# Layer 0 transposes the raw x, applies the inverse norm behind its projection, and takes x, identity and gain from one tensor

## The reference

```python
h = rms_norm(x, attn_norm[0])            # x * rsqrt(mean(x^2) + EPS) * gain, per token
proj = h @ w_in                          # q, k, v (1024 columns each) and 16 forget-gate columns
q = rms_norm(proj[..., :D] per head, qn)
k = rms_norm(proj[..., D:2*D] per head, kn)
v = proj[..., 2*D:3*D]
log_f = log_sigmoid(proj[..., 3*D:] + b_f)
cum = cumsum(log_f) over tokens          # enters the attention logits
```

## Time and profile before

| | us |
|---|---|
| median of 3 runs | 1317.16 |
| lowest and highest | 1314.86, 1318.45 |
| the profiled execution, its own time | 1315.91 |
| its span | 1314.1 |
| PE busy in it | 1295.5 |
| DVE, ACT, POOL busy | 1008.7, 873.4, 458.7 |

### The profile page before, as it was taken

One profiled execution on the slowest core, in us unless ns is written; L12 is line 12 of the kernel. 1 busy time (PEld: TensorE's weight loads), 2 busy tenths in 40 slices (PEclk: granted clock), 3 DMA queues, 4 the chain that ended last, 5 costly groups with the idle time before them and its releaser, 6 DMA issues.

```text
span 1314.1 us, 22109 instructions
## 1 busy us (share of the span) xinstructions
PE 1295.5 (99%) x6964; PEld 1096.7 (83%) x6964; DVE 1008.7 (77%) x1603; ACT 873.4 (66%) x1567; POOL 458.7 (35%) x498
## 2 busy tenths in 40 slices
PE   7999999999999999999998999999999999999998
PEld 5888888888888888888887888888888888888887
DVE  6877898955777788885578789886476888888745
ACT  6776777744667777774467777775367776777533
POOL 3741245410275225552026314552015521555200
PEclk9999999999999999999998999999999999999999
DMA  7734555565664455556451365556455435555651
GB/s 268 237 102 141 174 192 185 189 219 166 203 228 146 148 180 180 191 190 216 168 185 61 115 211 192 187 184 211 163 198 187 144 113 189 183 189 192 213 171 64
DMA packets 64602, 232.39 MB, mean 177 GB/s; under 512 B 7472, under 2 KB 7600, under 8 KB 64528
## 3 DMA queue, kind: packets, MB, share of 16 engines
q1 hardware_dynamic: 61632, 221.35, 50.7%
q0 software_dynamic: 2896, 10.08, 2.5%
HBM read 230.35 MB, written 1.05 MB: 176 GB/s over the span
## 4 chain that ended last, share of the span: by engine, by line
PE 97%; DVE 1%; ACT 1%; DMA 0%; issue 0%; POOL 0%; SPq 0%; DVEq 0%
PE bank L1589 28%; PE bank L1895 25%; PE bank L1898 12%; PE bank L1565 7%; PE bank L1567 6%; PE bank L1566 6%; PE bank L1604 5%; PE bank L1736 2%; PE bank L1759 2%; PE bank L1575 2%; PE bank L1658 1%; DMA w_raw<-weights 0%; PE bank L1683 0%; PE bank L1744 0%; ACT w_hi L457 0%
## 5 line engine op out<-in xcount | busy, mean ns | idle before, releaser
L866 DVE TENSOR_TENSOR w_lo<-w_raw,w_hi 128x1024 fp32r<-128x1024 f32 x418 | 543.3, 1318 | 109.2 <-ACT w_hi L457 107.7
L457 ACT ACTIVATE w_hi<-w_raw 128x1024 fp32r<-128x1024 f32 x418 | 430.2, 1053 | 136.5 <-PE bank L1589 107.5
L1895 PE MATMUL bank<-hT,w_hi 128*128 128x512 f32 x1408 | 444.6, 395 | 0.0
L1898 PEld LDWEIGHTS bank<-hT,w_lo 128*128 128x128 f32 x1408 | 264.5, 188 | 59.7
L1898 PE MATMUL bank<-hT,w_lo 128*128 128x256 f32 x1408 | 281.9, 278 | 0.0
L1550 POOL TENSOR_TENSOR gT_lo<-gate_c,gT_hi 128x256 f32 (+1 forms) x88 | 170.8, 1941 | 201.8 <-ACT gT_hi L818 201.8
L1895 PEld LDWEIGHTS bank<-hT,w_hi 128*128 128x128 f32 x1408 | 216.6, 189 | 3.9 <-issue 1.1
L1381 POOL TENSOR_SCALAR ssq<-ssq 128x1 f32<-128x1 f32 x24 | 12.7, 528 | 361.9 <-ACT tok L483 361.9
L1565 PE MATMUL bank<-w_hi,hT 128*128 128x512 f32 (+1 forms) x336 | 134.3, 400 | 2.0 <-DVE hT L920 2.0
L1567 PE MATMUL bank<-w_hi,hT 128*128 128x512 f32 (+1 forms) x336 | 130.5, 388 | 0.0
L1566 PE MATMUL bank<-w_lo,hT 128*128 128x512 f32 (+1 forms) x336 | 130.4, 388 | 0.0
(11 more groups left out here) (164 smaller groups left out, 1991.1 us busy)
## 6 DMA issues: line engine op xcount, KB each, us to landing
w_raw<-weights SPq DMA_DIRECT2D x418, 512.0 KB, 3.7
gain<-gains POOLq DMA_DIRECT2D x11, 512.0 KB, 4.6
rel<-rel_in POOLq DMA_DIRECT2D x8, 256.0 KB, 4.0
x<-x_in SPq DMA_DIRECT2D x4, 256.0 KB, 4.3
out<-x SPq DMA_DIRECT2D x4, 256.0 KB, 2.0
p_end<-p_in POOLq DMA_DIRECT2D x3, 256.0 KB, 4.9
consts<-consts_in POOLq DMA_DIRECT2D x1, 392.0 KB, 5.2
conv_sb<-conv POOLq DMA_DIRECT2D x1, 352.0 KB, 3.8
```

The lines of the kernel that those rows point to most:

```text
L457: nc.scalar.activation(w_hi[:, slot, q * HALF:(q + 1) * HALF], w_raw[:, raw, :], ACT.Copy).then_inc(hi_ready, 1)
L866: nc.vector.tensor_tensor(w_lo[:, slot, cols], w_raw[:, half(q)[0], :], w_hi[:, slot, cols].bitcast(F32), ALU.subtract).then_inc(lo_ready, 1)
L1895: nc.tensor.matmul(up_banks(L, slot)[:, side, :], w_hi[:, *at(side)], hT[:, c, :, :], start=c == 0, stop=c == KC - 1, skip_group_check=True)
L1898: last = nc.tensor.matmul(up_banks(L, slot)[:, side, 0:SEQ], w_lo[:, *at(side)], hT_hi[:, c, :], start=False, stop=c == KC - 1, skip_group ...
```

## The change

Layer 0's first norm loses its multiplication. PE transposes the raw `x`; ACT and DVE still apply the gain behind the transposes. The inverse norm `rstd` (one number for each token) is applied when q, k and v are copied out of PSUM, as a per-partition scale of the ACT copies (`rstd` for L572 and L587, `rstd_sq` = `rstd` / 8 for the squares of L575), and in the v rest. `rstd_sq` is made by two new POOL instructions ahead of POOL's DMA issues. For the forget gate, whose result has heads on partitions, PE also transposes a broadcast of `rstd` (two more transposes) and DVE multiplies by it (`gate_in` has five instructions instead of two).

Identity, gain and x become one tensor in DRAM (`first_ins`, 8768 bytes a partition row) and one in SBUF (`first_in`); the first of the four x transfers brings gain, identity and 512 columns of x in rows of 2624 bytes, and SP issues two DMAs fewer ahead of the weights. ACT and DVE change order at the start: rounding comes before the split of the same step, the squares of both tiles come after the second unit's split, and tile 1's rounding is interleaved with the fourth unit's halves. The gain buffer's first load no longer waits. `first_in` is 1 KB longer per partition than x was; with `ident`, `gain0` and `qr` gone as tensors of their own, everything placed behind the old `ident` lies 512 bytes higher, and x, tok, hT and gain 1024 bytes; w_raw, w_hi and w_lo stay. `qr` moves into `small`.

```diff
+X_AT = 256
+GAIN0_AT = X_AT - KC - P - 8
-        x = sb("x", [P, TT, D])
+        first_in = sb("first_in", [P, X_AT + TT * D])
+        gain0 = first_in[:, GAIN0_AT:GAIN0_AT + KC]
+        ident = first_in[:, GAIN0_AT + KC:GAIN0_AT + KC + P]
+        x = first_in[:, X_AT:X_AT + TT * D].rearrange("p (t d) -> p t d", t=TT)
...
 # SP
-                    c = slice(b * 512, (b + 1) * 512)
-                    sp.dma_start(x[:, t, c], x_in[t * P:(t + 1) * P, c]).then_inc(x_landed[2 * t + b], 16)
-                if t == 0:
-                    sp.dma_start(ident[:], ident_in).then_inc(ident_landed, 16)
-                    sp.dma_start(gain0[:], gain0_in).then_inc(gain0_landed, 16)
+                    c = slice(X_AT + t * D + b * 512 if t or b else GAIN0_AT, X_AT + t * D + (b + 1) * 512)
+                    sp.dma_start(first_in[:, c], first_ins[:, c.start - GAIN0_AT:c.stop - GAIN0_AT]).then_inc(x_landed[2 * t + b], 16)
...
 # ACT
+            for b in range(2):
+                round_hT(0, 0, parts=(b,))
+                split_hi(0, 0, half_of(0), first=True, halves=(b,))
+            split_hi(1, 1, half_of(1), first=True)
             square(0, 0)
-            for b in range(2):
-                split_hi(0, 0, half_of(0), first=True, halves=(b,))
-                round_hT(0, 0, parts=(b,))
-            split_hi(1, 1, half_of(1), first=True)
             square(0, 1)
             split_hi(2, 2, half_of(2), first=True)
-            split_hi(3, 3, half_of(3), first=True, halves=(0,))
-            round_hT(0, 1)
-            split_hi(3, 3, half_of(3), first=True, halves=(1,))
+            for b in range(2):
+                round_hT(0, 1, parts=(b,))
+                split_hi(3, 3, half_of(3), first=True, halves=(b,))
...
+                    if L == 0:
+                        act.wait_ge(rstd_sq_ready, t + 1)
+                    nc.scalar.activation(qn[:, n % 3, 0:cols], src[:, 0:cols], ACT.Copy,
+                                         scale=1.0 if L else rstd[:, t:t + 1]).then_inc(raw_ready, 1)
+                    nc.scalar.activation(sq[:, 0:cols], src[:, 0:cols], ACT.Square,
+                                         scale=HD ** -0.5 if L else rstd_sq[:, t:t + 1]).then_inc(sq_ready, 1)
...
 # DVE
-            dve.wait_ge(x_landed[0], 16)
-            dve.wait_ge(x_landed[1], 16)
-            normalise(0, 0)
-            dve.wait_ge(gain0_landed, 16)
             for b in range(2):
+                rest_hT(0, 0, parts=(b,))
                 split_lo(0, 0, half_of(0), halves=(b,))
-                rest_hT(0, 0, parts=(b,))
             split_lo(1, 1, half_of(1))
-            normalise(0, 1)
             split_lo(2, 2, half_of(2))
-            split_lo(3, 3, half_of(3), halves=(0,))
-            rest_hT(0, 1)
-            split_lo(3, 3, half_of(3), halves=(1,))
+            for b in range(2):
+                rest_hT(0, 1, parts=(b,))
+                split_lo(3, 3, half_of(3), halves=(b,))
...
+                    if L == 0:
+                        dve.wait_ge(f_done, 1)
+                        own.inc(nc.vector.tensor_copy(fe[:], aux[1][0:HEADS, SEQ:2 * SEQ]))
+                        own.inc(nc.vector.tensor_scalar(fmin[:], aux[1][2 * HEADS:3 * HEADS, 0:SEQ], 0.0, None, ALU.add))
+                        own.wait()
+                        own.inc(nc.vector.tensor_tensor(fz[:], aux[1][0:HEADS, 0:SEQ], fmin[:], ALU.add))
+                        own.wait()
+                        own.inc(nc.vector.tensor_tensor(fmin[:], fz[:], fe[:], ALU.mult))
+                        own.wait()
+                        nc.vector.tensor_scalar(fz[:], fmin[:], bf[:, 0:1], None, ALU.add).then_inc(f_z, 1)
+                        return
...
 # POOL
             norm_rstd(0)
+            for t in range(TT):
+                pool.wait_ge(rstd_ready, t + 1)
+                nc.gpsimd.tensor_scalar(rstd_sq[:, t:t + 1], rstd[:, t:t + 1], HD ** -0.5, 1.0, ALU.mult, ALU.mult).then_inc(rstd_sq_ready, 1)
             pool.dma_start(p_raw(0), p_in[0]).then_inc(p_landed, 16)
...
 # PE
+                    if L == 0:
+                        pe.wait_ge(rstd_ready, TT)
+                        for t in range(TT):
+                            nc.tensor.transpose(aux[1][0:HEADS, SEQ + t * P:SEQ + (t + 1) * P],
+                                                       rstd[:, t:t + 1].to_broadcast([P, HEADS]), ident)
```

More of the change, by code:

```diff
@@ L153, in half_of, with trunk @@
     return lambda q: ((2 * u + q) % RAW, (2 * u + q) // RAW + 1)
-def trunk(nc, weights, x_in, p_in, gains, gain0_in, smalls, gainT_in, bf_in, conv, wf_in, rel_in, ident_in, consts_in, out):
+def trunk(nc, weights, first_ins, p_in, gains, smalls, gainT_in, bf_in, conv, wf_in, rel_in, consts_in, out):
     with ExitStack() as ctx:
@@ L169, in trunk @@
         gain = sb("gain", [P, D])
-        ident = sb("ident", [P, P])
         consts = sb("consts", [P, C_END])
@@ L255, in trunk @@
         sink = small[:, S_SINK:S_END]
+        qr = small[:, S_GAIN:S_GAIN + TT * HEADS].rearrange("p (t h) -> p t h", t=TT)
         def in_bank(i, t):
@@ L316, in trunk @@
         rstd_ready = sem("rstd_ready")
+        rstd_sq_ready = sem("rstd_sq_ready")
         tok_ready = sem("tok_ready")
@@ L586, in evacuate_v @@
                     wait_block(act, L, blk, t)
-                    nc.scalar.activation(v_hi[:, t, c * 512:(c + 1) * 512], in_bank(blk, t)[:, :], ACT.Copy).then_inc(v_hi_ready, 1)
+                    nc.scalar.activation(v_hi[:, t, c * 512:(c + 1) * 512], in_bank(blk, t)[:, :], ACT.Copy,
+                                         scale=1.0 if L else rstd[:, t:t + 1]).then_inc(v_hi_ready, 1)
                 def gate_logs():
@@ L902, in normalise @@
                 dve.wait_ge(rstd_ready, 2 * n + t + 1)
-                if n:
-                    dve.wait_ge(gain_landed, 16 * n)
+                dve.wait_ge(gain_landed, 16 * n)
                 for b in range(2):
                     c = slice(b * 512, (b + 1) * 512)
-                    if n == 0:
-                        nc.vector.tensor_scalar(tok[:, t, c], x[:, t, c], rstd[:, t:t + 1], None, ALU.mult).then_inc(tok_ready, 1)
-                        continue
                     nc.vector.scalar_tensor_tensor(tok[:, t, c], x[:, t, c], rstd[:, t:t + 1], gain[:, c],
@@ L1049, in rest_v @@
                         cols = slice(c * 512, (c + 1) * 512)
-                        ins = nc.vector.tensor_tensor(v_lo[:, t, cols], src[:, :], v_hi[:, t, cols].bitcast(F32), ALU.subtract)
+                        if L == 0:
+                            ins = nc.vector.scalar_tensor_tensor(v_lo[:, t, cols], src[:, :], rstd[:, t:t + 1],
+                                                                 v_hi[:, t, cols].bitcast(F32), ALU.mult, ALU.subtract)
+                        else:
+                            ins = nc.vector.tensor_tensor(v_lo[:, t, cols], src[:, :], v_hi[:, t, cols].bitcast(F32), ALU.subtract)
                     else:
@@ L1365, in load_gain @@
             def load_gain(n):
-                pool.wait_ge(tok_ready, 4 * n)
+                if n > 1:
+                    pool.wait_ge(tok_ready, 4 * (n - 1))
                 pool.dma_start(gain[:], bass.AP(gains.tensor, n * D, [[0, P], [1, D]])).then_inc(gain_landed, 16)
@@ L1571, in transpose_tok @@
                 for b in range(2):
-                    pe.wait_ge(tok_ready, 4 * n + 2 * t + b + 1)
+                    if n:
+                        pe.wait_ge(tok_ready, 4 * (n - 1) + 2 * t + b + 1)
+                    else:
+                        pe.wait_ge(x_landed[2 * t + b], 16)
                     for c in range(4):
@@ L1657, in transpose_items @@
                         for c in range(item_place(m, i)[3]):
-                            last = nc.tensor.transpose(item_bank(m, i)[:, c * P:(c + 1) * P], qn[:, n % 3, c * P:(c + 1) * P], ident[:])
+                            last = nc.tensor.transpose(item_bank(m, i)[:, c * P:(c + 1) * P], qn[:, n % 3, c * P:(c + 1) * P], ident)
                         last.then_inc(qk_tr, 1)
@@ L1758, in transpose_p @@
                     for c in range(3):
-                        last = nc.tensor.transpose(pt_bank(h)[:, c * P:(c + 1) * P], sc(m, h)[:, c * P:(c + 1) * P], ident[:])
+                        last = nc.tensor.transpose(pt_bank(h)[:, c * P:(c + 1) * P], sc(m, h)[:, c * P:(c + 1) * P], ident)
                     last.then_inc(pt_done, 1)
```

19 lines of the change are left out of this document (5 added, 14 removed).

## The result

The changed kernel takes 1319.67 us (median of 22 runs, 1316.73 to 1322.46) beside 1317.13 of the kernel before (22 runs, 1314.86 to 1320.19). The ratio is 1.0022 with a 95% interval of 1.0016 to 1.0028: 2.9 us more by the ratio, 2.1 to 3.7 by its interval. With so many runs the difference is clear of noise, yet it is within the 0.3% that the prediction calls no change. Predicted were 1317.2, in a range of 1312.5 to 1320.5.

A forecast was written before the change was run, and what follows sets the result against it. TensorE, busy in 99% of the span, was taken to bound the kernel. -2.2 us at the first matmul, +1.33 by 23 us, +0.25 for two transposes and +1.25 at item 5 gave +0.6 to +0.7: 1317.2, range 1312.5 to 1320.5.

The forecast's parts named there:

- rival E: Start: transfer-bound first weights still land at about 7, nothing gained there, later slip costs 2.0 us: 1319; chance 0.05.
- Start: Before the first matmul: weights issued 0.94 us earlier, first half unit landing at 6.0, matmul at 8.55: 2.2 us gained.
- Back to the last half unit: Next 15 us: ACT and DVE splits delay unit 3's last half, taken at 22.9; of 2.2 us gained, 0.87 left.
- The clock, and tile 1's transposes: Start: if TensorE's clock rises later against the first matmul, tile 1's transposes come later, losing up to 0.5 us more.
- POOL's queue: POOL's DMA issues start at 16.9 instead of 15.82, 1.1 us later, behind tile 1's squares and two new instructions.
- Item 0 on ACT: Layer 0, ACT waiting for gainT: all of POOL's 1.1 us slip arrives, item 0 near 27.2.
- Pointer scales: Layer 0's ACT copies: 0.684 us instead of 0.597, costing 0.2 us for item 1 and 0.5 for later items.
- The gate: Forget gate on DVE: five instructions instead of two, 1.3 us longer, bounds 0.9 and 1.8.
- Item 5: POOL's chain in layer 0: ready 2.9 us later, at 62.8; TensorE waits 1.25 us, going on 0.7 later than before.
- Sum at the first scores: After item 5, TensorE runs without pause, so +0.7 us goes through to the end.
- The shift: SBUF buffers 512 bytes higher: taken as costing nothing, since no row tells instructions apart by address.
- rivals C and D: Layer 2's attention: C, clock doesn't fall, 1312.5, chance 0.13; D, clock low for longer, 1321.4, chance 0.10.

The follow-up runs named there:

- e4: The kernel before with only the changed kernel's SBUF layout, all DMAs and instructions as they were: 1318.04 us, ratio 1.0003.
- e6: The kernel before with 32 unused bytes per partition behind nsink and nothing else: 1324.19 us, ratio 1.0048.
- e10: The kernel before with 64 unused bytes per partition behind nsink: 1323.97 us, ratio 1.0048.
- e11: The kernel before with 32 unused bytes ahead of qT_hi, gT_hi and gT_lo as before: 1317.62 us, ratio 1.0001.
- e12: The kernel before with 32 unused bytes ahead of gT_lo and 32 more ahead of up_c: 1322.36 us, ratio 1.0034.
- e7: The changed kernel with the edits of e1 and e2, and tile 0's squares in ACT's wait for the first weights: 1316.78 us, ratio 0.9996.
- e9: e7 with all four first weight halves issued ahead of tile 1's x pieces: 1316.90 us, ratio 0.9997.
- e3: The kernel before with only the merged x, gain and identity transfer and new SP order, old norm, buffers shifted 480 bytes: 1324.15 us, ratio 1.0051.
- e5: e3 with 32 bytes of pad, making the shift 512, and qr moved into small: 1317.06 us, ratio 1.0000.
- e8: The changed kernel with the gate's sum as before, without its multiplication by rstd: 1318.24 us, ratio 1.0002.
- e2: The changed kernel with tile 1's roundings and rests and the last unit's halves in the old order: 1319.74 us, ratio 1.0017.
- e1: The changed kernel with POOL's two rstd_sq instructions moved behind its DMA issues: 1317.26 us, ratio 1.0000.

## Why the prediction was right, and where its sizes weren't

The time came out inside the stated range, 0.8 us below its upper end, and each step has the sign that was forecast; but single steps are up to four times off, and the errors partly cancel. That is in part luck. One of the prediction's own signs of being wrong came true: the first half unit landed after 6.8 us, as rival E has it, and E's time of 1319 is nearer to the 1319.67 than the forecast of 1317.2; E's "nothing is gained" at the first matmul did not come true. In the order of the prediction's steps:

- **Start, -2.2 us forecast, -0.87 measured.** x landed at 3.72 and was off the path, as said. The first half unit landed at 7.53, not at 6.0, and this is the whole error of this term. Its landing scatters: 7.21 to 8.50 in the six kernels that load in the old order (before, e4, e6, e10, e11, e12), 5.86 to 7.60 in the eight of the new (for e7 and e9, where ACT comes later, from the issue and the time to landing, 6.76 and 6.66). The medians are 7.69 and 6.75, so the 0.94 us of earlier issue arrive whole at the landing: from issue to landing it takes 5.1 us in the median in either order, 4.2 to 5.9 in single kernels. The changed kernel's 5.8 is at one end of this scatter, and the 4.3 that I took at the other. Rival E's condition (later than 6.8) was met in three of the eight. The 0.2 us for a smoother transfer had no ground: the dip that I put down to the identity and the gain is there in all eight kernels without these two transfers, between 5 and 6 us and with 143 to 262 GB/s. In the changed kernel (columns as in the earlier trace rows):

```profile
5.00:6.00 1.00, 0.69 (x4) 0.28 (x2) 0.00 (x0) 1.00 (x4) 0.00 (x0) 1.00 0.84 205
```

In e3 and e5 the first matmul came at 10.56 and 10.57, though their weights landed at 6.74 and 5.86: with the old way through the norm that way ends last, and the merge brings 0.2.
- **Back to the last half unit, +1.33 forecast, +1.69 measured** (-0.87 to +0.82). The two waits are there (0.36 and 0.51 us), set by DVE's split of that half (23.31, forecast 21.6). ACT took the fourth half at 12.68, when it landed, and not at 11.5, and later it stood 0.83 us for tile 1's transposes (next point). The +0.82 also makes the change look worse than it is: e4 and e6 start as the kernel before does, and take this half at 24.40 and 24.31, not 23.77.
- **The clock, and tile 1's transposes.** I had set up to 0.5 us on a rise of the clock that comes late against the first matmul. The matmuls shortened from 0.63 to 0.40 us between 15.6 and 16.0 us, 5.7 to 6.1 us after the first one instead of 4.8 to 5.1, so this case arrived. (The granted clock reads 1.00 in all windows of the start, so I take the two levels from the pace: 0.43 us from start to start for 512 columns, then 0.23, that is 1.2 GHz and about twice that.) The first matmul was late too, so tile 1's transposes came at 18.29, and ACT waited for them. In e8, which has the same order on ACT and DVE, the first matmul came at 9.01 and the transposes at 17.31, and ACT had no wait. First the changed kernel, then e8:

```profile
18.29 1.03 PE L1591 MATMUL bank<-first_in 128*128 128x128 f32 x8
18.92 1.14 ACT L494 ACTIVATE hT<-bank,first_in 128x128 fp32r<-128x128 f32 x4 [0.83 <-PE bank L1591]
```

```profile
17.31 1.03 PE L1580 MATMUL bank<-first_in 128*128 128x128 f32 x8
17.95 1.14 ACT L494 ACTIVATE hT<-bank,first_in 128x128 fp32r<-128x128 f32 x4
```

From ACT's first split of unit 2 (16.10, 15.98, 16.13) to DVE's split of the last half (23.31, 22.54, 22.69) it takes 7.21 us in the changed kernel and 6.56 in e8 and in e2. e2 has the old order, a first matmul as late (9.97) and an early clock (13.1 us, transposes at 17.05). So late transposes cost the changed kernel 0.65 us, and the 0.64 by which e2 takes the last half earlier are no price of the new order by itself: in e8 it costs nothing. That the rise came at about the time of before (15.61) is a coincidence: in e9 it was 12.7 to 13.1 and in e11 17.4 to 17.7, with first matmuls at 9.56 and 11.68.
- **POOL's queue, +1.1 us forecast, +3.71 measured** (15.82 to 19.53). This is the term that was mis-sized most. 1.38 us of it is the wait for tile 1's squares, which ended later (17.20 instead of 15.82; I had 0.34), and 2.33 are the two `rstd_sq` instructions, to which I gave 0.3 us each: they took 2.38 together, beside two of DVE's splits (17.17, 2.36 us), which read two SBUF operands. In e1, beside DVE's `hT` rests (one of whose two tensors is in PSUM), they took 0.37, and in e7, where one split was half over, 0.92.
The Trainium skill ("SBUF — State Buffer", who interferes with whom) says that a DVE instruction with two SBUF inputs contends with a GpSimd one that reads SBUF, and that the loser stands until the other has ended. The trace agrees: the two last 1.17 and 1.25 us, a split 1.18 (2.36 / 2).
- **Item 0 on ACT, +1.1 forecast, +3.16 measured** (26.07 to 29.23): the slip did arrive whole, less 0.55 us.
- **Pointer scales.** In the means, ACT's copies for q, k and v with a pointer scale take 0.68 us and those without 0.60, as the earlier trace rows said.
- **The gate, +1.3 forecast, +1.85 measured** (0.92 to 2.77). Four of the five run at 0.34 to 0.42; the product (L1064, two SBUF operands) took 1.07, from 48.52 on, and ended 0.27 behind POOL's `qn` (48.27 to 49.32), which fits a wait for it.
- **Item 5: ready +5.04 instead of +2.9.** These are item 0's 3.16 and the gate's 1.85. Whatever the start gained ahead of it was lost here, as e2 shows. The forecast wait of 1.25 us was measured as 1.14, but the agreement is partly chance: POOL came 2.1 us later than forecast, and TensorE too (63.83 by 64.97 less its wait, not 61.5). Item 1, which "just fits", missed by 0.31.
- **Sum at the first scores, +0.7 forecast, +2.87 measured.** It is 0.82 at the last half unit, 0.2 for the two transposes, 0.47 at item 1 (the wait of 0.31 and its restart), 1.3 at item 5, with less than 0.1 left over. Of the forecast's own range (1315 to 1319) the median lies 0.7 us outside.
- **The shift, nothing.** Right for this shift as far as e4 and e5 can tell (to 1.2 us either way), wrong in its reason. I argued that no row tells instructions apart by address; shifts of 32, 64 and 480 bytes cost 7 us each.
- **Layer 2, rivals C and D.** In the window of the earlier trace rows the changed kernel shows a higher mean clock than before:

```profile
712.00:726.00 14.00, 9.88 (x62) 8.11 (x64) 11.48 (x48) 11.82 (x41) 8.25 (x16) 0.75 0.09 31
```

It comes to this place 2.85 us later, so the window doesn't cover the same work; at 715 to 729 us the mean is 0.65. The granted clock was 0.50 at 715.8 to 719 and again at 722.7 to 729.3, some 10 us in two pieces, where the kernel before had some 14 in one. And still the stretch took 0.35 us longer: the gain of C did not come, nor the loss of D. The other kernels show how this place scatters. From layer 1's first up matmul to layer 2's it takes 303.22 to 304.44 us in the ten kernels whose down matmuls are at 389 ns, with some 10, 14 or 17 us at half the clock; the stretches from layer 0's to layer 1's, from layer 2's to layer 3's and from there to the last transposes each agree within 0.22 us. So the 0.35 is inside the scatter. e1's execution has the 17 us and the 304.44, so at 1319.16, the longest of e1's eleven, it ends only 0.2 us ahead of the changed kernel's, though it was 1.03 ahead at the scores.

What stays open: how much of e1's gain is real (2.41 us by the medians, 1.03 by the traces; the interval of e1's ratio is 1.2 us either way), what makes the first half unit's landing scatter (of the old order, the three at 8.03 to 8.50 ran on another chip than e4 and e6, but e9, on that chip too, is not late), when the clock changes, and how the operands' addresses act. Tried were shifts of everything by 32, 64 and 480 (slow) and of 512 (free), of `gT_lo` and `gate_c` by 32 with `up_c` and the buffers behind it by 64 (slow), and of q, k, v, pT and qn by 32 (free); 128 and 256 weren't tried.

## What to carry to other kernels

Work taken off the critical path at the start isn't gone: look for the engine queue in which it now stands, and what is issued behind it. Here the small instructions were better placed behind the DMA issues of their queue, and the squares in a gap in which ACT waited anyway; together with the old order of tile 1's roundings this turned 2.9 us of loss into none that can be told. When a buffer is added or resized, keep the addresses of the matmuls' operands where they were or test the shift by itself: compare the mean duration of each matmul group before looking for any other cause. And before a number from one trace is explained, look at how far kernels with the same code in that stretch lie apart: here 1.5 us at the first scores and 1.2 us in layer 2.

## What the runs showed of the hardware

- 32 bytes more ahead of the operands made the down projection's matmuls 395 to 396 ns long instead of 389, 1324.19 us instead of 1317.25; 512 bytes did nothing that can be told.
- A single-column POOL instruction took 0.21 to 0.22 us in e1 and 1.17 to 1.25 us in the changed kernel beside DVE's splits with two SBUF operands (0.37 and 2.38 for two).
- The moment of the first clock rise did not follow the kernel's first matmul: 12.7 us in e9, 15.6 in before and e6, 17.4 in e11, and between about 3 and 6 us after the first matmul in all of them. The matmuls show it in these rows of e9:

```profile
12.28 0.63 PE L1579 MATMUL bank<-w_hi,hT 128*128 128x512 f32 x1
12.71 0.55 PE L1580 MATMUL bank<-w_lo,hT 128*128 128x512 f32 x1
13.10 0.39 PE L1581 MATMUL bank<-w_hi,hT 128*128 128x512 f32 x1
```

The Trainium skill ("TensorE: Matmul & The Clock Gate", the HAM clock gate) says that this moment varies from run to run. These numbers fit that, though each is one execution of another kernel.
- The first half unit of the weights landed between 5.86 and 7.60 us in eight kernels that issue it at 1.66 us, and between 7.21 and 8.50 in six that issue it at 2.60: 4.2 to 5.9 us after the issue in both.
